# Fused two-block decoder on one core: recurrence ends overlapped, two norms made one, delta-rule slots regrouped

## The reference, cut to what matters

```python
# first block, layer 1: 16 heads of 64; one step for each token
r, k, v = einsum('nbsd,nde->nbse', stack([xr, xk, xv]), w_rkv)
w = -softplus(-(w0 + tanh(xw @ w1) @ w2)) - 0.5
a = sigmoid(a0 + (xa @ a1) @ a2);  g = sigmoid(xg @ g1) @ g2
y = _wkv7_scan(r, exp(-exp(w)), k, v, -kk, kk * ah)     # recurrence over tokens
out = ((groupnorm(y) * ln_w + ln_b + bonus) * g) @ w_o
x = x + gt1 * out;  x = x + gt2 * mlp(modulate(rmsnorm(x)))
return _rmsnorm(x, final_g)                             # closing norm

# second block, layer 0: hn = rms_norm(h, attn_norm); 8 heads of 128
qkv, z, b_raw, a_raw = split(hn @ w_in)                 # conv of width 4, silu, l2 norm
def step(state, inp):                                   # 8 chunks of 64 tokens, in order
    v_new = ui - einsum('bhck,bhkv->bhcv', wi, state)
    o = einsum(qd, state) + einsum(ai, v_new)
    state = state * exp(gl) + einsum('bhck,bhcv->bhkv', kd, v_new)
o = rms_norm(o, o_gain) * silu(z);  h = h + o @ w_out
```

## Time and profile before

| | us |
|---|---|
| median of 3 runs | 3247.34 (3246.79 to 3247.5) |
| profiled execution | 3245.51 |
| its span in the profile | 3243.7 |

### The profile page before, as it was taken

The page is one execution under the profiler, slowest core; times in us unless marked ns, Lnnn a source line. Parts: engine busy times, 40 slices in busy tenths (PEclk is TensorE's granted clock), DMA queues, the critical chain, the costliest instruction groups (busy, mean ns, idle before and its releaser), DMA issues.

```text
span 3243.7 us, 47867 instructions
## 1 busy us (share of the span) xinstructions
PE 2960.1 (91%) x21522; PEld 2377.9 (73%) x21522; DVE 1564.2 (48%) x2190; ACT 1075.3 (33%) x1405; POOL 197.5 (6%) x163
## 2 busy tenths in 40 slices
PE   4999999699799978999689999889999897789999
PEld 4877888568688867888466666578888684578887
DVE  6666553563577644332446565543333655443332
ACT  3225233343233225233333232232222556432221
POOL 1010000200322100000100000010000000000000
PEclk9999999899899989999889999689999998999999
DMA  7444543111000022222111111022322220022321
GB/s 268 182 182 156 194 177 129 57 68 39 25 4 3 3 105 87 95 95 94 55 65 40 40 40 35 6 78 79 109 96 93 78 79 1 39 90 72 118 88 62
DMA packets 41580, 269.72 MB, mean 83 GB/s; under 512 B 4256, under 2 KB 4384, under 8 KB 13344
## 3 DMA queue, kind: packets, MB, share of 16 engines
q1 hardware_dynamic: 39504, 260.93, 22.5%
q10 hardware_dynamic: 1872, 5.74, 0.5%
HBM read 264.55 MB, written 2.10 MB: 82 GB/s over the span
## 4 chain that ended last, share of the span: by engine, by line
PE 84%; DVE 8%; ACT 5%; DMA 1%; issue 1%; POOL 1%; SPq 0%; POOLq 0%; DVEq 0%; ACTq 0%
PE ps L595 20%; PE ps L597 20%; PE ps L602 20%; PE ps L1860 6%; PE ps L2584 1%; PE ps L1462 1%; PE ps L1479 1%; PE ps L1473 1%; PE ps L2017 1%; DMA W<-w_ada 1%; PE ps L2019 1%; PE ps L2005 1%; DVE WL L409 1%; PE ps L1949 1%; POOL ACC L496 1%
## 5 line engine op out<-in xcount | busy, mean ns | idle before, releaser
L595 PE MATMUL ps<-HH,WH 128*128 128x512 f32 x1928 | 768.1, 398 | 53.6 <-ACT HH L571 39.9
L597 PE MATMUL ps<-HH,WL 128*128 128x512 f32 x1928 | 758.7, 394 | 0.0
L602 PE MATMUL ps<-HL,WH 128*128 128x512 f32 x1928 | 736.0, 393 | 1.7 <-DVE HL L552 1.7
L409 DVE TENSOR_TENSOR WL<-ST,WH 128x2048 fp32r<-128x2048 f32 (+2 forms) x227 | 461.7, 2035 | 260.1 <-ACT WH L401 259.8
L401 ACT ACTIVATE WH<-ST 128x2048 fp32r<-128x2048 f32 (+2 forms) x211 | 382.6, 1813 | 318.6 <-PE ps L602 294.9
L595 PEld LDWEIGHTS ps<-HH,WH 128*128 128x128 f32 x1928 | 368.0, 191 | 142.5 <-issue 64.7
L602 PEld LDWEIGHTS ps<-HL,WH 128*128 128x128 f32 x1928 | 366.4, 190 | 82.0 <-DVE HL L552 4.5
L597 PEld LDWEIGHTS ps<-HH,WL 128*128 128x128 f32 x1928 | 368.0, 191 | 78.8 <-issue 2.9
L595 PE MATMUL ps<-GH,WH 128*128 128x512 f32 x928 | 361.6, 390 | 0.0
L597 PE MATMUL ps<-GH,WL 128*128 128x512 f32 x928 | 361.0, 389 | 0.0
L602 PE MATMUL ps<-GL,WH 128*128 128x512 f32 x928 | 359.8, 389 | 0.0
(11 more groups left out here) (344 smaller groups left out, 3776.9 us busy)
## 6 DMA issues: line engine op xcount, KB each, us to landing
ST<-w_m SPq DMA_DIRECT2D x64, 1024.0 KB, 4.9
ST<-w_gu SPq DMA_DIRECT2D x44, 1024.0 KB, 4.7
ST<-w_ada SPq DMA_DIRECT2D x40, 1024.0 KB, 6.3
ST<-w_dn SPq DMA_DIRECT2D x32, 704.0 KB, 4.1
ST<-w_gin SPq DMA_DIRECT2D x16, 1024.0 KB, 4.7
ST<-w_cin SPq DMA_DIRECT2D x12, 1024.0 KB, 4.9
ST<-w_rkv SPq DMA_DIRECT2D x12, 1024.0 KB, 4.7
ST<-w_kv SPq DMA_DIRECT2D x8, 1024.0 KB, 4.8
```

Source lines behind the costliest of these rows:

```text
L409: o = e.tensor_tensor(WL[:, j % 3, cut], ST[:, pos % 3, cut], WH[:, j % 3, cut].bitcast(F32), ALU.subtract)
L595: e.matmul(big.tile((tag, m))[:, :], wh[:, k, c0:c0 + P], H[:, k, :], start=(k == 0), stop=False)
L597: e.matmul(big.tile((tag, m))[:, :], wl[:, k, c0:c0 + P], H[:, k, :], start=False, stop=False)
L602: o = e.matmul(big.tile((tag, m))[:, :], wh[:, k, c0:c0 + P], L[:, k, :], start=False, stop=(k == kt - 1))
```

## The change

It has five parts. New line numbers are those of the changed kernel.

- **Start of the recurrence.** The first five steps of pre(0) are taken on every engine while v is being projected: on TensorE the decay and gate products after v tile 2 and ss after tile 4, on ACT behind the copies of the v tiles, on DVE behind its own part of v. The small weights and tables they need are loaded before the LoRA layers. `first_b` gives them banks 6, 7, 5. Buffers are placed anew in the weight buffers' room.
- **End of the recurrence.** SP loads the first piece of wo once product g of m = 7 is done, the second after y0 and mq of m = 7. ACT and DVE make WH and WL (in four quarters) beside the copies of the last post. TensorE takes 18 products of wo before the mean of m = 7 and 24 behind it; `tensor_dense` then begins at k = 7.
- **One norm.** ACT squares X for `final` and, scaled by sqrt(final_g^2 + 1e-6), for `attn0` beside it, and POOL adds both. `attn0` needs no scaled X: its gain is final_g times attn_norm, its epsilon 1e-12. X is scaled after the decay's cumulative sum. 24 project steps of head 0 stand between ab and the rows.
- **Slots of the delta rule.** A slot is one back step, one front step, then one or two project steps (3 or 6 products); 32 project steps of 21 slots run on across heads, so that 8 of them are left over for the last segment. The state is kept for every c, so nothing waits for o1; o1 (L2152) and o2 (L2158) come as two batches of 8 after the last ws. silu of z moves one head on, the table load goes ahead of the output's squares.
- **End of the delta rule.** 42 products of gout (k = 0 to 6) stand in the last head's slots 7, 9, ... 19.

```diff
...
+            for t in squares_of(tag):
+                scale = 1.0
+                if t == "attn0":
+                    scale = SM[:, 56 + k:57 + k]
+                    e.wait_ge(*norm_vec.at("both", "root"))
+                if k:
+                    e.wait_ge(*tmp.free(("square", t, k)))
+                e.activation(tmp.tile(("square", t, k)) if k else sums_of(t)[:, :], X[:, k, :], ACT.Square,
+                             scale=scale).then_inc(*square.up(t, k))
 
...
+        def tensor_group(e, tag, n, group, k, H, L, high, low):
+
+            j = J[tag][n]
+            _, kt, c = shape(j)
+            wh, wl = halves(j)
+            first = n * (c // P)
+            if k == 0:
+                for m in group:
+                    e.wait_ge(*big.free((tag, m)))
+            if n == 0:
+                e.wait_ge(*high(k))
+            for m in group:
+                ps, cs = big.tile((tag, m)), slice(P * (m - first), P * (m - first) + P)
+                e.matmul(ps[:, :], wh[:, k, cs], H[:, k, :], start=(k == 0), stop=False)
+                e.matmul(ps[:, :], wl[:, k, cs], H[:, k, :], start=False, stop=False)
+            if n == 0:
+                e.wait_ge(*low(k))
+            for m in group:
+                ps, cs = big.tile((tag, m)), slice(P * (m - first), P * (m - first) + P)
+                o = e.matmul(ps[:, :], wh[:, k, cs], L[:, k, :], start=False, stop=(k == kt - 1))
+                if k == kt - 1:
+                    o.then_inc(*mm.up(tag, m))
+
+        def tensor_dense(e, tag, H, L, high, low, after=None, hooked=True, begun=0):
...
+                for group in ([tiles] if n == 0 else [[m] for m in tiles]):
+                    for k in range(0 if n else begun, kt):
+                        tensor_group(e, tag, n, group, k, H, L, high, low)
+                    if after and hooked:
+                        for m in group:
...
+            pre = tensor_pre(e, 0)
             for tag in "rkv":
-                tensor_dense(e, tag, HH, HL, split_high("mix" + tag), split_low("mix" + tag))
+                tensor_dense(e, tag, HH, HL, split_high("mix" + tag), split_low("mix" + tag),
+                             lambda m: next(pre) if 1 < m < 2 + AHEAD else None, tag == "v")
+            return {("pre", 0): pre}
...
+            for n, at_ in ((0, 1), (0, 2), (0, 3), (0, 4), (1, 15), (2, 16), (2, 17)):
+                out.insert(len(out) - POST + at_, ("wo", n))
+            return out[AHEAD:]
+
...
+        def tensor_wo(e, n):
+            if n < 2:
+                return
+            e.wait_ge(*lo.at(J["wo"][0]))
+            for k in range(3):
+                tensor_group(e, "wo", 0, [0, 1], k, HH, HL, scan_high, scan_low)
+            yield
+            for k in range(3, 7):
+                tensor_group(e, "wo", 0, [0, 1], k, HH, HL, scan_high, scan_low)
+            yield
+
+        def scalar_wo(e, n):
+            if n == 0:
+                e.wait_ge(*scan_mm.at("y0", 6))
+            else:
+                e.wait_ge(*scan_mm.at("y0", 7))
+            if n < 2:
+                scalar_take(e, ("early", n))
+            for _ in range(4):
+                yield
+
+        def vector_wo(e, n):
+            if n == 0:
+                for part in range(4):
+                    vector_low(e, J["wo"][0], part, 4)
+                    yield
+
         def scan_high(k):
...
         def tensor_rwkv(e):
-            tensor_projections(e)
+            begun = tensor_projections(e)
             e.wait_ge(*out_act.at("v", 7))
             in_turn(RWKV, {"pre": lambda m: tensor_pre(e, m), "inv": lambda m: tensor_inv(e, m),
-                           "post": lambda m: tensor_post(e, m)})
-            e.wait_ge(*scan_vec.at("low", 7))
+                           "post": lambda m: tensor_post(e, m), "wo": lambda n: tensor_wo(e, n)}, begun)
             tensor_columns(e, ("need", "wo"))
-            tensor_dense(e, "wo", HH, HL, scan_high, scan_low)
+            tensor_dense(e, "wo", HH, HL, scan_high, scan_low, begun=7)
 
...
 
 
-            out = [("project", 0)] * GDN_PROJECT
+            ahead_ = [("project", h) for h in range(8) for _ in range(GDN_PROJECT)]
+            out, ahead_ = ahead_[:24], ahead_[24:]
             for h in range(9):
-                steps = []
-                if h:
-                    steps += [((i + 0.5) / GDN_BACK, 0, "head", h - 1) for i in range(GDN_BACK)]
-                if h < 7:
-                    steps += [((i + 0.5) / GDN_PROJECT, 1, "project", h + 1) for i in range(GDN_PROJECT)]
-                if h < 8:
-                    steps += [((i + 0.5) / GDN_FRONT, 2, "head", h) for i in range(GDN_FRONT)]
-                    steps += [((i + 0.9) / 6, 3, "low", (h, i)) for i in range(6)]
-                else:
-                    steps += [((i + 0.7) / 8, 3, "split", i) for i in range(7)]
-                out += [(kind, n) for _, _, kind, n in sorted(steps)]
+                for i in range(GDN_FRONT):
+                    if h and i < GDN_BACK:
+                        out.append(("head", h - 1))
+                    if h < 8:
+                        out.append(("head", h))
+                    n = (i + 1) * GDN_PROJECT // GDN_FRONT - i * GDN_PROJECT // GDN_FRONT
+                    out, ahead_ = out + ahead_[:n], ahead_[n:]
+                    if h < 8 and i % 3 == 2:
+                        out.append(("low", (h, i)))
+                    if h == 8:
+                        if i % 2 == 0 and i < 14:
+                            out.append(("split", i // 2))
+                        if i % 2 and i > 6:
+                            out.append(("gout", 0))
             return out + [("split", 7)]
...
-            e.wait_ge(*gdn_pool.at("zero", h))
-            e.wait_ge(*gdn_b.free(("o1", h)))
-            e.wait_ge(*gdn_b.free(("o2", h)))
-            po1, po2 = gdn_b.tile(("o1", h)), gdn_b.tile(("o2", h))
             for c in range(8):
                 c2, p = c // 2, c % 2
-                cs = slice(64 * c, 64 * c + 64)
                 if c:
                     e.wait_ge(*gdn_vec.at("s", h, c - 1))
                     e.wait_ge(*gdn_act.at("wt", h, p))
                     e.wait_ge(*gdn_b.free(("ws", h, c)))
-                    e.matmul(gdn_b.tile(("ws", h, c))[rows(p), 0:P], WT[:, cs], SG[:, :], start=True,
+                    e.matmul(gdn_b.tile(("ws", h, c))[rows(p), 0:P], WT[:, 64 * c:64 * c + 64], SG[:, c, :], start=True,
                              stop=True).then_inc(*gdn_mm.up("ws", h, c))
-                o = e.matmul(po1[rows(p), P * c2:P * c2 + P], QK[:, 0, cs], SG[:, :], start=True, stop=True)
-                if c == 7:
-                    o.then_inc(*gdn_mm.up("o1", h))
-                elif c:
-                    o.then_inc(*gdn_mm.up("read", h, c))
-                if c:
                     yield
-                e.wait_ge(*(gdn_vec.at("vn", h, c) if c else gdn_vec.at("us", h)))
                 if c < 7:
+                    e.wait_ge(*(gdn_vec.at("vn", h, c) if c else gdn_vec.at("us", h)))
                     e.wait_ge(*gdn_b.free(("s", h, c)))
                     e.matmul(gdn_b.tile(("s", h, c))[:, 0:P], KD[rows(p), c2, :], XV[rows(p), c2, :], start=True,
                              stop=True).then_inc(*gdn_mm.up("s", h, c))
-                o = e.matmul(po2[rows(p), P * c2:P * c2 + P], AL[rows(p), c2, 0:64], XV[rows(p), c2, :], start=True,
-                             stop=True)
-                if c == 7:
-                    o.then_inc(*gdn_mm.up("o2", h))
-                yield
+                    yield
+            e.wait_ge(*gdn_pool.at("zero"))
+            e.wait_ge(*gdn_b.free(("o1", h)))
+            for c in range(8):
+                o = e.matmul(gdn_b.tile(("o1", h))[rows(c % 2), P * (c // 2):P * (c // 2) + P],
+                             QK[:, 0, 64 * c:64 * c + 64], SG[:, c, :], start=True, stop=True)
+            o.then_inc(*gdn_mm.up("o1", h))
+            e.wait_ge(*gdn_b.free(("o2", h)))
+            e.wait_ge(*gdn_vec.at("vn", h, 7))
+            for c2, p in PAIRS:
+                o = e.matmul(gdn_b.tile(("o2", h))[rows(p), P * c2:P * c2 + P], AL[rows(p), c2, 0:64],
+                             XV[rows(p), c2, :], start=True, stop=True)
+            o.then_inc(*gdn_mm.up("o2", h))
...
+        def tensor_gout(e):
+
+            e.wait_ge(*lo.at(J["gout"][0]))
+            e.wait_ge(*gdn_act.at("raw", 7, 3))
+            for k in range(7):
+                tensor_group(e, "gout", 0, [0, 1], k, HH, HL, out_high, out_low)
+                yield
+
         def tensor_gdn(e):
+            project = tensor_project(e, 0)
+            tensor_rms(e, "attn0", EX)
+            tensor_dense(e, "ab", HH, HL, split_high("attn0"), split_low("attn0"))
             tensor_rms(e, "final")
-            tensor_rms(e, "attn0")
-            tensor_dense(e, "ab", HH, HL, split_high("attn0"), split_low("attn0"))
+            in_turn(GDN[:24], {"project": lambda h: project})
             ps = sml.tile(("gc",))
```

(17 more changed lines are left out.)

406 lines of the change are left out of this document (234 added, 172 removed).

## The result

| | us |
|---|---|
| before, median of 4 runs | 3247.07 (3245.44 to 3247.5) |
| after, median of 4 runs | 3218.61 (3217.64 to 3221.58) |
| ratio after to before | 0.9915, 95% interval 0.9898 to 0.9932 |
| span of the profiled execution, after | 3216.2 (before 3243.7) |

The time lies outside the stated range (3143 to 3197), above it. The two traces can be laid side by side at seven points that both kernels have. Nearly all of the difference to the forecast is in one line.

What follows compares the result with a forecast made beforehand. TensorE, busy 91% of the span, bounds the kernel. −16.7 − 15 − 32.7 − 8 + 2 − 7 = −77.4 on 3245.5 gives 3168.1; the median is 1.8 above, rounded down to 3169 us. Range 3143 to 3197.

Steps and rivals of the forecast that it cites:

- Start: Start of the recurrence: early steps taken while v is projected bring gb 14.2 us earlier, 2.5 more from the clock; −16.7 us.
- end: End of the recurrence: wo's products cover the wait for the mean, its first group ends 15.0 us sooner; −15 us.
- last head: Head 7's back: 42 products of gout move into waits of DVE and ACT; −7 us (−10 to −2).
- One norm: Between the blocks: second norm drops out, head 0's products fill the stretch before the rows; −32.7 us (27 to 36).
- Slots of the delta rule: Six heads, u to u: fewer small-step groups and batched o1, o2 against new waits; 52.7 us a head, −8 in all.
- The lower bound: A delta rule head without the new waits: 53.97 − 4.5 = 49.4 us.
- where a WL half (about 1.2) stands ahead of vn: 0.6 per head: Delta rule slots: the next step waits for DVE, with 3 products (0.7 us) as cover; 0.6 us per head.
- Rival 3: Delta rule falls to the lower clock for good: 31 us a head, 3356 us, slower than before; chance 0.02.
- Rival 2: Waits grow, each slot showing a piece of ws, vn, s or conv: 56 us a head, 3198 up to 3230; chance 0.13.
- Rival 1: Slots bound by TensorE alone: six heads take 49.4 us each, last front gains too, 3147 us; chance 0.13.
- The prediction's signs: Changed trace: head 52 to 53 us, wait of 1 us or more before the front step behind the sums, clock 1.0.
- The rule on tiling modes: Delta rule: any tiling mode change drains TensorE, also between adjacent back and front steps; head 53.4 us, sum 3173.

Runs made afterwards that it cites:

- e8: Changed kernel with AHEAD = 0, so no step of pre(0) is taken while v is projected, early loads kept: 3225.87 us, ratio 0.9936.
- e7: Kernel of e2 with a project step between s and the sums in slot 7 and the WL half of slot 8 and later ones moved later: 3159.7 us.
- e1: Changed kernel with DVE's halves of WL in slots 0, 3, 6, ... of a head instead of 2, 5, 8, ...: 3213.33 us, ratio 0.9892.
- e2: Changed kernel with 28 project steps of head 0 ahead of the rows instead of 24, so z and WH come earlier: 3182.0 us, ratio 0.9791.
- f1: Kernel of e7 with 24 project steps ahead of the rows again instead of 28: 3205.09 us, ratio 0.9869.
- e3: Changed kernel with the delta rule's list merged by position as before, kept states and batches of o1 and o2 staying: 3175.02 us, ratio 0.9774.
- e4: Kernel before the change with the six low steps of each head at (i + 0.15) / 6 instead of (i + 0.9) / 6: 3249.84 us, ratio 1.0006.
- e5: Kernel of e2 with one project step between s and the sums in slot 7 of each head: 3181.36 us, ratio 0.9801.
- f4: Kernel of e7 with the small root's tensor_scalar and the product behind it written as scalar_tensor_tensor: 3158.73 us, ratio 0.9727.

## Why the prediction was wrong, point by point

- **Start, end, last head: right in size.** −18.1 for −16.7, −14.1 for −15, −6.1 for −7. For gb 814.3 was forecast, 813.99 measured, and e8 shows both parts of it, the loads and the steps taken ahead. The end has its steps as described, with one size off: the first quarter of WL waits 2.83 us for WH (1130.89), so that the last m became 3.8 longer, not 2.35. That was the first sign of what went wrong in the heads. Counted from the steady steps, the mean came 2.9 us later than forecast and the stretch ended only 0.9 short of it, so that 2 us of its size came from elsewhere and the nearness of the total is partly luck. The last front was +0.2 for +2.
- **One norm: right, at the small end.** ab's start fell as forecast (7.7 behind the norm). But the rows came 8.4 and not 14.1 earlier than the MLP's end would have them: TensorE waits 3.55 us for a copy of ACT within the 24 project steps, and 4.95 for ACT's squares of head 0 later (1.40 in the kernel before), with DVE's convolution as the pace. The prediction named that cover and priced it at 3 to 5; the stretch fell short by 3.7. The waits are 7.1 us more, so that 3.4 were gained back at places that were not followed up.
- **Slots of the delta rule: the failed step.** The lower bound stood: 49.4, and 49.45 measured in e7. The step that failed first is "where a WL half (about 1.2) stands ahead of vn: 0.6 per head". I counted DVE's own time of the half and not what it waits for. WH is made by ACT behind the copy of z, and z now ends in slot 5, where a `low` step stands. In the list both can be seen: 24 steps ahead leave 8 for a head's z, and the 8th falls into slot 5. The price was 3.6 us of waiting for TensorE, not 0.6; the rows of e1, e2 and f1 show it from three sides. ot cost 0.6 for 0.4, t0 1.43 for 2.3; these were right or too high, so that all waits together were 5.8 for 3.3, only 2.5 more.
- **The clock was priced at nothing, and that is the larger part.** The sum of a head, 49.4 + 3.3, has no term for it. Rival 3 had it as a matter of the whole delta rule or none. In fact it fell for a part of each head: 61.49 − 49.4 − 5.8 leaves 6.3 us a head for it, of the 8.8 by which this head is above 52.7. "Rounded down with the clock, which can only gain a little in the stretches that are now filled" was wrong in the heads. The argument against rival 3, that the clock of before falls only behind waits of microseconds, was a misreading: the stretch of the earlier trace rows has none ahead of it. Taken together, the wait for WH and the clock behind it cost 6.1 (e2) to 6.85 us (f1) of the 8.9 a head, and the two leftovers, mostly through the clock, the rest.
- **The rivals.** Rival 2 (the waits grow) had the right sign, with a price of +20 for six heads; it was +53 against my 52.7 a head (61.6 − 52.7 = 8.9, times 6). Its mechanism, a piece in every slot, was not what happened: one wait and the clock behind it did most of it. Rival 1 (49.4 throughout, 3147) is not reached when the wait is taken away, but e7 comes between it and the forecast: 51.95 a head, 50.8 at the full clock, 3159.7. The prediction's signs name no single long wait in a head, which is what the trace shows.
- **The rule on tiling modes** (the Trainium skill, TensorEngine Tiling (Array Packing), Key Properties). By it the changes between two small steps would have cost 0.7 a head more, 50.1 of TensorE's own time. e7's head at the full clock has 49.45, and e3's, with the old order of the list and the same batches, has 50.30. e3 has 25 groups of small steps in a head and e7 22, so three groups fewer saved 0.85, where 0.2 each was counted and nothing by the rule. The measurement goes by the groups alone.

## What to carry to other kernels

When a list is merged anew, ask of every instruction that moves not only how long it takes but whose result it waits for, and where that maker stands in its own queue. The same half of WL at the same place ahead of vn cost nothing when its WH had been made before (e2), and 6.85 us a head when WH came late (f1); a shorter wait with little due behind it cost nothing (e4). And where TensorE works close to its limit, price a wait of some microseconds twice: with 3.6 us of standing still came 3.1 us of lower clock. Read the clock of every head of before, too, and not of one good one.

## What the runs showed of the hardware

- The granted clock fell to its lower level (products 0.43 us apart) behind waits of 3.6 us, and in e2 behind 3.3 us of small products in a row with no wait in it. In the kernel before it fell in such a row too, for 8 us of the products behind it, with no wait of 0.2 us or more in the 20 us ahead. Separating those products alone moved the lower stretch behind the next wait of 1.43 us in three of six heads (e5); shortening that wait too, to 0.95, left three of six heads at 1.00 (e7). What exactly decides in the others is open.
- DVE's operation on 128x4 elements started 0.03 us behind POOL's product on 128x512 and took 1.27 us as tensor_scalar and 1.26 as scalar_tensor_tensor, against 0.16 to 0.17 alone (e7, f4). Of these two forms neither was a way out; no other was run. The Trainium skill, SBUF — State Buffer, Who interferes with whom, says that the two engines share a pair of ports as an exclusive lock; a DVE operation with two SBUF inputs needs it while GpSimd reads SBUF, and tensor_scalar can enter a mode that takes both of DVE's ports. Both rows agree with it, the scalar_tensor_tensor by its two inputs and the tensor_scalar if it was in that mode, which no row shows.
